# A two-layer decoder step on one core: zero-padding short contractions of the gated linear attention to 128 rows, and summing squares between the layers two tiles at a time

## What is computed

```
h = h + rms_norm(mix @ w_out, post_g)                    # end of layer 0
z = rms_norm(h, pre_g) @ w_in                            # start of layer 1
q, k, v, gate, lr = jnp.split(z, ODD_SPLITS, axis=-1)    # lr: 16 wide
g = jax.nn.log_sigmoid((lr @ wa2 + ba)) / GLA_TAU        # decay logits, contraction over 16
...
state = (jnp.exp(b_last)[..., None] * state
         + jnp.einsum('bhsd,bhse->bhde', kc * jnp.exp(b_last - b), vc))   # per chunk of tokens
```

## Time and profile before

| what | value |
|---|---|
| runs: median of 3 (lowest to highest) | 2025.7 us (2025.2 to 2025.81) |
| the profiled execution: its own time | 2029.64 us |
| its span, first to last instruction | 2027.7 us |
| mean granted TensorE clock over the span | 0.975 |
| PE busy | 1961.5 us, 97% of the span |
| the boundary, from the end of layer 0's sums to the first head's chunk | about 995 to 1049 us of the span |
| the four heads | about 1049 to 1815 us of the span |

### The profile page before, as it was taken

The page is one execution under the profiler, slowest core; times in us unless marked ns, Lnnn a source line. Parts: engine busy times, 40 slices in busy tenths (PEclk is TensorE's granted clock), DMA queues, the critical chain, the costliest instruction groups (busy, mean ns, idle before and its releaser), DMA issues.

```text
span 2027.7 us, 38550 instructions
## 1 busy us (share of the span) xinstructions
PE 1961.5 (97%) x15065; PEld 1845.0 (91%) x15065; DVE 835.6 (41%) x1469; ACT 641.9 (32%) x1156; POOL 689.0 (34%) x304
## 2 busy tenths in 40 slices
PE   6999999999999999999899999999999999989999
PEld 6998998899889988999779989988998899879999
DVE  5366338534852676000351365054406532650003
ACT  5132223222321324222242343233324422442213
POOL 2333233233323322545314224323342333224551
PEclk8999999999999999999899999998999899979999
DMA  6554345434533453532234453434344424544232
GB/s 203 164 163 129 103 116 158 124 91 126 168 106 97 134 152 117 157 88 84 82 103 116 125 159 92 126 120 162 84 126 146 138 82 120 177 137 133 84 93 96
DMA packets 357436, 252.55 MB, mean 125 GB/s; under 512 B 15135, under 2 KB 324784, under 8 KB 356720
## 3 DMA queue, kind: packets, MB, share of 16 engines
q1 hardware_dynamic: 316194, 186.70, 32.1%
q10 hardware_dynamic: 41070, 63.46, 9.3%
HBM read 213.62 MB, written 36.96 MB: 124 GB/s over the span
## 4 chain that ended last, share of the span: by engine, by line
PE 85%; DVE 8%; issue 4%; ACT 2%; DMA 1%; POOL 0%; ACTq 0%; DVEq 0%; SPq 0%; POOLq 0%
PE proj L1003 70%; PE scratch L1003 9%; PE score L1003 3%; PE scratch L1006 2%; DVE kv L1551 1%; PE proj L1006 1%; DVE xlo L1425 1%; DVE xlo L1423 1%; DVE ek L1822 1%; DVE probw L1579 1%; DVE el L1818 0%; DVE tz L1412 0%; DVE sall L1554 0%; DMA xin<-in_x_prompt 0%; ACT ek L862 0%
## 5 line engine op out<-in xcount | busy, mean ns | idle before, releaser
L1003 PE MATMUL proj<-xhi,wlo 128*128 128x268 f32 x4096 | 1198.3, 293 | 17.2 <-DVE xlo L1425 7.5
L1003 PE MATMUL proj<-xlo,whi 128*128 128x268 f32 x4096 | 1187.1, 290 | 0.0
L1003 PE MATMUL proj<-xhi,whi 128*128 128x268 f32 x4096 | 1186.9, 290 | 0.0
L547 POOL TENSOR_TENSOR wlo<-wraw,whi 128x1024 fp32r<-128x1024 f32 x258 | 635.5, 2473 | 1101.3 <-ACT whi L613 1101.3
L1003 PEld LDWEIGHTS proj<-xhi,wlo 128*128 128x128 f32 x4096 | 787.2, 192 | 38.8 <-issue 23.1
L1003 PEld LDWEIGHTS proj<-xlo,whi 128*128 128x128 f32 x4096 | 786.5, 192 | 0.7
L1003 PEld LDWEIGHTS proj<-xhi,whi 128*128 128x128 f32 x4096 | 783.4, 191 | 0.0
L613 ACT ACTIVATE whi<-wraw 128x1024 fp32r<-128x1024 f32 x258 | 265.0, 1046 | 381.1 <-PE proj L1003 275.6
L1730 DVE TENSOR_SCALAR mix<-proj,cols 128x536 f32 x32 | 24.8, 775 | 341.2 <-ACT te L619 177.8
L1412 DVE TENSOR_TENSOR tz<-proj,rstd 128x536 f32<-128x536 f32 x72 | 51.3, 713 | 236.4 <-PE proj L1003 235.4
L728 ACT ACTIVATE probw<-score,small 128x128 f32<-128x128 f32 (+3 forms) x64 | 33.2, 523 | 173.7 <-DVE small L1502 173.7
(11 more groups left out here) (286 smaller groups left out, 1756.5 us busy)
## 6 DMA issues: line engine op xcount, KB each, us to landing
wraw<-in_w_in SPq DMA_DIRECT2D x192, 512.0 KB, 4.1
wraw<-in_w_out SPq DMA_DIRECT2D x64, 512.0 KB, 4.1
kv<-in_cache_k SPq DMA_DIRECT2D x128, 128.0 KB, 2.3
kv<-in_cache_v SPq DMA_DIRECT2D x128, 128.0 KB, 2.3
sst<-in_state_gla ACTq DMA_DIRECT2D x32, 512.0 KB, 4.9
out<-sst ACTq DMA_DIRECT2D x32, 512.0 KB, 3.5
hbuf<-h_residual ACTq DMA_DIRECT2D x2, 4288.0 KB, 14.8
vb<-v_sample_rows ACTq DMA_DIRECT2D x32, 256.0 KB, 5.5
```

Of the source, the lines that this page charges most:

```text
L547: pool.tensor_tensor(wlo[:, slot, :, 0:width], wraw[:, kc, :, 0:width], whi[:, slot, :, 0:width].bitcast(F32), ALU.subtract).then_inc(s_lo, 1)
L1003: return pe.matmul(out, lhsT, rhs, start=start, stop=stop, skip_group_check=True)
```

## The change

Three parts. First, the contraction over 16 rows is done over 128 rows with zeros in the other 112: `lrT` and `wa2` grow to 128 partitions and are cleared by DVE (SP's first fetch of `wa2` waits for that, semaphore `s_wpad`); the last chunk's keys go to a tile of their own, `kdt`, cleared once, and the last slice of `gv` is cleared once, so SU40 and SU41 run over 128 rows. Second, in the boundary loop PE does the `lr` and value matmuls of each k first and, after each odd k, adds up the squares of both tiles of the pair: four matmuls with 32 columns of ones (two halves, two tiles), each to its own 32 partitions of `score`; ACT squares a tile one step later than before. Third, what the four groups hold has to be put together: ACT copies the 128x268 sums to `gsum`, and PE spreads them with a matrix of 1/32 and 0 (`spread`, written by DVE in 8 pieces) by two matmuls, before `finish_rms(2)`.

```diff
--- before.py
+++ after.py
@@ -206,6 +206,7 @@
         s_xhi, s_x = sem("s_xhi"), sem("s_x")
         s_sq, s_acc = sem("s_sq"), sem("s_acc")
         s_ss, s_rstd = sem("s_ss"), sem("s_rstd")
+        s_gsum = sem("s_gsum")
         s_hst, s_hld = sem("s_hst"), sem("s_hld")
         s_yt, s_hn = sem("s_yt"), sem("s_hn")
         s_yout = [sem("s_yout"), sem("s_yout_first")]
@@ -290,7 +291,7 @@
         fac_ready = sig("factors_ready", ("head", chunks, GH))
         ed_exp = sig("ed_exp", ("head", chunks[1:], GH))
         ed_ready = sig("ed_ready", ("head", chunks[1:], GH))
-        s_c0, s_wa2, s_cols = sem("s_c0"), sem("s_wa2"), sem("s_cols")
+        s_c0, s_wa2, s_cols, s_wpad = sem("s_c0"), sem("s_wa2"), sem("s_cols"), sem("s_wpad")
         s_maskr = sem("s_maskr")
         s_vs, s_vb = sem("s_vs"), [sem("s_vb0"), sem("s_vb1")]
         s_st, s_sdec, s_snew = [sem("s_st0"), sem("s_st1")], sem("s_sdec"), sem("s_snew")
@@ -350,14 +351,15 @@
         hbuf = sb1("hbuf", [P, KT, T])
         acc = sb1("acc", [P, T])
         ybuf = sb1("ybuf", [P, 11, 4, P])
+        spread, gsum = ybuf[:, 0, 0:2, :], acc[:, 0:TH]
         stage.close()
         stage = ExitStack()
         lower = sb1("lower", [P, n_second])
         fold = lower[:, P:P + NB]
         qd = sb1("qd", [P, 2, 32 * NB])
         srow = tef[:, 0:GV]
-        lrT = sb1("lrT", [RANK, T])
-        wa2 = sb1("wa2", [RANK, GK])
+        lrT = sb1("lrT", [P, T])
+        wa2 = sb1("wa2", [P, GK])
         gq = sb1("gq", [P, 2, T])
         gk = sb1("gk", [P, 2, T])
         gb = sb1("gb", [P, 2, T])
@@ -367,6 +369,7 @@
         ed = sb1("ed", [P, 2, P])
         el = sb1("el", [P, 2, P])
         kd = sb1("kd", [P, GK])
+        kdt = sb1("kdt", [P, GK])
         st = sb1("st", [P, P])
         state = sb1("state", [P, 2, GV])
         og = sb1("og", [P, 4, T])
@@ -511,9 +514,10 @@
                     load(N_HEAD + c // 2 + 12 * s, c % 2, w_in1, head_col(c // 2, s))
                     if c == 2:
                         sp.wait_ge(s_hn, KT)
+                        sp.wait_ge(s_wpad, 1)
                         src = A["gla_wa2_1"][:, bass.ds((s + 1) * GK - GK, GK)]
                         sp.wait_ge(*freed_back("head", "G11", s))
-                        sp.dma_start(wa2[:], src).then_inc(s_wa2, 16)
+                        sp.dma_start(wa2[0:RANK, :], src).then_inc(s_wa2, 16)
 
             with sp.Fori(0, GH) as s:
                 head(s)
@@ -835,7 +839,11 @@
                 act.wait_ge(s_hn, k + 1)
                 act.dma_start(h_dram[1, k], mix[:, k, :]).then_inc(s_hst, 16)
                 act.activation(xhi[:, k, :], mix[:, k, :], ACT.Copy, scale=cols[:, PRE1 + k:PRE1 + k + 1]).then_inc(s_xhi, 1)
-                square(2, k % 2, k, mix[:, k, :])
+                if k:
+                    square(2, (k - 1) % 2, k - 1, mix[:, k - 1, :])
+            square(2, 1, KT - 1, mix[:, KT - 1, :])
+            act.wait_ge(s_acc, 2 * KT)
+            act.copy(gsum, score[:, 0:TH]).then_inc(s_gsum, 1)
             act.dma_start(lower[:], A["lower"]).then_inc(s_c1, 16)
             finish_rms(2)
             act.wait_ge(s_hst, 16 + 16 * KT)
@@ -1240,10 +1248,6 @@
             pe.wait_ge(*free_d.before("head", BY_DVE["head"][0], 0))
             pe.wait_ge(s_lo, 2 * N_LR + 4)
             for k in range(KT):
-                pe.wait_ge(s_sq, KT + k + 1)
-                for a in range(2):
-                    last = matmul(score2[:, a, 0:TH], ones, (tz, te)[k % 2][:, a, :], start=k == 0, stop=k == KT - 1)
-                last.then_inc(s_acc, 1)
                 pe.wait_ge(s_x, X_SPLIT["in1"] + k + 1)
                 w = (k // HC, k % HC)
                 for a in range(2):
@@ -1260,9 +1264,19 @@
                     matmul(out, wlo[:, 2 + w[0], w[1], :], xhi[:, k, x], start=k == 0, stop=False)
                     matmul(out, whi[:, 2 + w[0], w[1], :], xlo[:, k, x], start=False, stop=False)
                     last = matmul(out, whi[:, 2 + w[0], w[1], :], xhi[:, k, x], start=False, stop=k == KT - 1)
-            last.then_inc(s_tile, 1)
-            pe.wait_ge(s_acc, 2 * KT)
-            pe.sem_inc(s_ss, 1)
+                if k == KT - 1:
+                    last.then_inc(s_tile, 1)
+                if k % 2:
+                    pe.wait_ge(s_sq, KT + k + 1)
+                    for a in range(2):
+                        for j in range(2):
+                            r = 32 * (2 * j + a)
+                            last = matmul(score[r:r + 32, 0:TH], ones[:, 0:32], (tz, te)[j][:, a, :], start=k == 1, stop=k == KT - 1)
+                    last.then_inc(s_acc, 2)
+            pe.wait_ge(s_gsum, 1)
+            for a in range(2):
+                last = matmul(score2[:, a, 0:TH], spread[:, a, :], gsum)
+            last.then_inc(s_ss, 1)
 
             def head(s):
                 n0 = N_HEAD + 12 * s
@@ -1335,8 +1349,7 @@
                         done(last)
                     elif kind == "SU":
                         c, j = int(op[2]), int(op[3])
-                        w = P if c < TT else TAIL
-                        done(matmul(out[:, 0:GV], kd[0:w, j * P:(j + 1) * P], gv[0:w, c, :]))
+                        done(matmul(out[:, 0:GV], (kd if c < TT else kdt)[:, j * P:(j + 1) * P], gv[:, c, :]))
                     elif op == "SO":
                         pe.wait_ge(s_srow, s + 1)
                         for v in range(4):
@@ -1741,6 +1754,9 @@
                 dve.tensor_tensor(mix[:, k, :], mix[:, k, :], hbuf[:, k, :], ALU.add).then_inc(s_hn, 1)
 
             out_stage(1, N_OUT0, POST0)
+            for j in range(2):
+                for q in range(4):
+                    dve.memset(spread[32 * q:32 * q + 32, j, :], 1.0 / 32 if q % 2 == j else 0.0)
             dve.wait_ge(s_rstd, 2)
 
             dve.sem_inc(s_evac, 1)
@@ -1752,12 +1768,16 @@
                 if k >= 2:
                     x_lo("in1", k - 2, k - 1, PRE1)
 
+            dve.memset(wa2[:], 0.0).then_inc(s_wpad, 1)
             dve.wait_ge(s_rstd, 3)
+            dve.memset(lrT[:], 0.0)
             dve.memset(st[:], 0.0)
+            dve.memset(kdt[:], 0.0)
+            dve.memset(gv[:, TT, :], 0.0)
             link(dve.memset(qd[:], 0.0))
             dve.wait_ge(s_tile, N_LR + 3)
             for a in range(2):
-                dve.tensor_tensor(lrT[:, a * TH:(a + 1) * TH], scratch[a][0:RANK, 0:TH], rstd[0:RANK, a, :], ALU.mult).then_inc(s_lr, 1)
+                dve.tensor_tensor(lrT[0:RANK, a * TH:(a + 1) * TH], scratch[a][0:RANK, 0:TH], rstd[0:RANK, a, :], ALU.mult).then_inc(s_lr, 1)
             dve.wait_ge(s_c1, 16)
             dve.wait_ge(s_hst, 16 + 16 * KT)
 
@@ -1836,7 +1856,7 @@
                         m, n = (SUB * (i + 1), SUB) if c < TT else (TAIL, TAIL)
                         x = slice(SUB * i, SUB * i + n)
                         dve.tensor_tensor(st[0:m, x], src[0:m, x], lower[0:m, x], ALU.mult)
-                    dve.tensor_copy(kd[0:w, :], src[0:w, P:3 * P]).then_inc(s_fd, 1)
+                    dve.tensor_copy((kd if c < TT else kdt)[0:w, :], src[0:w, P:3 * P]).then_inc(s_fd, 1)
 
                 def update(c):
```

## The result

| what | before | after |
|---|---|---|
| runs: median (lowest to highest) | 2025.45 us of 4 (2024.77 to 2025.81) | 2001.62 us of 4 (2000.7 to 2008.46) |
| the profiled execution: own time, span | 2029.64, 2027.7 us | 2008.46, 2006.7 us |
| mean granted clock over the span | 0.975 | 0.981 |
| PE busy | 1961.5 us, 97% | 1936.7 us, 97% |

The changed kernel takes 0.989 of the time before, with a 95% interval of 0.9868 to 0.9912, so it is faster. (Of the experiments, one of six executions of x6_restart ran at a mean granted clock of 0.554 and is left out of its numbers.)

The account below looks back on a forecast made before the run. PE, busy for 1961.5 of 2027.7 us, was taken as the bound. Boundary 5.2, logits 1.7 and SU4 10.0 sum to 16.9 us, giving 2012.7 from the profiled execution, 2008.8 from the median; forecast 2010 us, range 2001 to 2021.

Parts of the forecast that it names:

- The squares of a pair: Boundary loop on PE: four column groups run together, 0.79 us a pair, bounds 0.45 and 1.78.
- Rival 2: Boundary squares: the four column groups run one after another, a pair takes 4.73 us; 2017.4 us in all, chance 0.05.
- The boundary's end: End of the boundary loop: ACT's logarithm starts 5.2 us earlier, at 1039.4 instead of 1044.62; bounds 6.5 and 3.
- the detour: Behind the last pair: ACT's copy 0.48 us, two spreading matmuls 0.89 us, handovers and a matmul's tail some 0.5 us.
- Edits at nothing: Clearings and the pieces of `spread` on DVE: fit into idle time, at worst delaying the loop up to 1 us.
- Logits: Decay logits of the first head: with 128 rows no clock fall behind them, 1.7 us gained, bounds 0 and 1.7.
- SU4: Padded last state update in four heads: 20.0 us less at half clock, so 10.0 us gained, bounds 16.8 and 3.4.
- Rival 1: Padded matmuls in the heads: zeros buy no clock, only the boundary gains; 2020.5 us, chance 0.10.
- Rival 3: Boundary loop: it never leaves half clock, logarithm 15.7 us late; slower, 2034 us, chance 0.05.

Follow-up runs that it names:

- x6_restart: Changed kernel plus 11 matmuls of ones behind the spreading matmuls, ahead of PE's restart; 2006.0 us, ratio 0.9893 to the kernel before.
- x4: Changed kernel with its pairs' squares added up by 128 columns of ones, without column groups, copy and spreading matmuls; 2010.49 us, ratio 0.9932 to the kernel before.
- x3: Kernel before with only the decay logits' lrT and wa2 padded to 128 rows; 2022.96 us, ratio 0.9984.
- x1_boundary: Changed kernel with the zero-padding taken out, so the boundary part alone; 2017.96 us, ratio 0.9971 to the kernel before.
- x2: Kernel before with only the last state update SU4 padded to 128 rows; 2013.22 us, ratio 0.9941.
- x7: Changed kernel plus 18 matmuls of ones behind layer 0's sums of squares, ahead of the loop; 2001.62 us, ratio 0.9879 to the kernel before.

## Why the prediction was right, step by step

The time of 2001.62 us is inside the range of 2001 to 2021, but only 0.6 us above its lower end. The forecast of 2010 was right in sign and mechanism and short in size: the gain was 23.8 us where the sum said 16.9 (21.2 in the profiled executions, 2029.64 - 2008.46).

- **The squares of a pair.** Forecast 0.79 us, measured 0.68. The row of B6 was the right one to take it from. Rival 2 (groups one after another) is out by the same rows and by x4's 4 x 0.45.
- **The boundary's end.** This step was off: 5.2 us were forecast, with bounds of 3 and 6.5, and it was 6.83, outside them. (The bounds do not follow from their own terms. Squares at 0.45 and DVE's pace give 1034.0 + 1.48 + 0.45 + 1.87 = 1037.8, which is 6.8 us ahead of 1044.62; seven pairs dearer by 0.45 leave about 2 of the 5.2.) The step that failed is the premise that the clock comes back at 1010.8 as before, 12.0 us behind the first row scaling. It made PE's sum (1037.5) the later end and DVE's pace (1036.3) the earlier one. The clock came back 9.1 us behind the row scaling, and DVE's pace decided: taken back by the 1.78 us by which layer 0 differs, the last pair's squares begin at 1035.42, and with their 0.68 they end at 1036.1. In x6_restart, where half clock did last 12.2 us, PE's pace held as forecast and the gain was 45.82 - 39.88 = 5.94 us. The rest is small: a pair took 3.65 us at PE's pace and not 3.74, and the detour 1.69 us from the end of the squares (1037.88 to 1039.57) and not 1.87.
- **Edits at nothing.** `spread` took 1.76 us, where at most 1.5 was estimated, and was done 0.51 us ahead of the row scale, and PE's restart came 4.91 us behind the logarithm as before. PE waited for POOL's `wlo` there and for no new name.
- **Logits.** Forecast 1.7, profile 1.48, runs 2.2 in x3.
- **SU4.** Forecast 10.0 us from 33.6 us at half clock going down to 13.6. The two profiles have 34.0 and 13.6, and the stretch from OC4 to the end is 10.3 us shorter on average over three profiles without and six with the padding. That the two numbers are so close is in part luck: half clock at OC4 and SU4 is 30.6 us on average in the three and 15.9 in the six, which is worth 7.4 us, and the rest lies in other falls and in the 3 us of x1_boundary that are open. The way there was another, too: not one short fall in every head, but in the profile after none in two and 6.7 us in the others. There the clock came back 5.5 us behind SU4's start (1767.4 - 1761.9), not within 3.4.
- **The rest of the 21.0.** The stretch to the end lost 14.5 us, and half clock accounts for nearly all of it: over the whole stretch it went from 54.5 to 27.3 us, and half of the difference is 13.6. Of these, 10.2 us are the falls at OC4 and SU4 (34.0 to 13.6) and 3.4 us are falls elsewhere (20.5 to 13.7), which the sum had put at nothing. They lie behind the sums at the heads' ends, among others, where PE waits for `gq`. No edit of the change stands there, and they came to between 10.2 and 20.5 us in the twelve profiles; so this part of the gain is, as far as these profiles tell, their luck.
- **Rival 1** (zeros buy no clock) is out by x2 and x3. The Trainium skill (TensorE: Matmul & The Clock Gate, Part 1) names how busy the engine has been and no rows of the array. The trace differs, and the measurement decides: PE is busy throughout in all eight stretches at OC4 here and in the earlier trace rows, and with zeros in the other 112 rows the half clock was less or gone.
- **Rival 3** (the boundary stays at half clock) is out: 1.00 from 1009.70 to 1037.90 with four-group squares and 16-column `lr` in every k.

## What to carry to other kernels

A short contraction that runs while PE is otherwise busy can cost more than its own time: if the clock falls behind it, filling the rows with zeros costs nothing in streaming (SU4 at half clock took 3.76 us with 16 rows and 3.78 with 128) and gives a part of the clock back, and where short and full contractions alternate it also saves the pauses between them (0.2 us a group here). Sums with a block of ones need only 32 columns, and four of them side by side took 0.68 us, where one over 128 columns takes 0.45. When an engine's work shrinks, work out the next engine's pace and take the later of the two ends in each part of the loop; a share of clock lost ahead of that engine is free as long as its pace stays the later end (here up to 10.2 us behind the loop's start, and no longer at 12.2).

## What the runs showed of the hardware that was not expected

- Full rows can be faster than short ones at the same clock: 0.67 us for a group of OC4 over 128 rows, 0.86 with 16 rows in between.
- Layer 0, up to the loop's first row scaling the same instructions in all twelve profiles but for the clearings of `spread` and x7's matmuls of ones, both in time in which their engine had been idle, took from 995.17 us (x4_wide) to 1000.58 us (the changed kernel). Half clock explains only a part: x2_update and x4_wide both had 23.9 us of it in the first 990 us and differ by 3.8 us. Single profiles of this kernel can't be compared to better than that without marks in the timeline.
- Where the half clock falls moves too: x1_boundary had 23.8 us of it at OC4 and SU4, the kernel before and x3_logits 34.0, with the same instructions there.
